# Seven half-size products for the first layer's projections, and the output gate's projection moved from the gated scan into the attention

## The chip, the cores and the metric

The kernel is one program on one core of a Trainium2 chip. Five engines work in it: TensorE (PE in the rows; PEld is its weight loads) multiplies matrices, VectorE (DVE), ScalarE (ACT) and GpSimd (POOL) work elementwise, and SyncE (SP) issues most of the DMAs. Each takes its instructions in order and waits on semaphores. The metric is the time of one execution in microseconds (us), the median of several runs. All data are fp32. An fp32 product leaves two records in the trace, so counts of records are twice the counts of products.

## What is computed

Two gated mixer layers are followed by a third block with state-space and delta-rule scans and an expert layer. The change touches the first half of the first layer, whose inputs are `x` (1024 tokens by 1024 channels) and one weight matrix:

```python
proj = jnp.einsum('bsd,df->bsf', h, w_in).astype(jnp.float32)
qa, ka, va, qb, kb, vb, lr_f, lr_b, gate = _split(
    proj, (A_WIDTH, A_WIDTH, A_WIDTH, B_K_WIDTH, B_K_WIDTH, B_V_WIDTH, B_GATE_RANK, B_GATE_RANK, MIX_WIDTH))
oa = dilated_attention(heads(qa, A_HEADS), heads(ka, A_HEADS), heads(va, A_HEADS), rel_bias)
g_f = jax.nn.log_sigmoid(lr_f @ up[0] + gb_[0]) / B_GATE_NORMALIZER
ob = bidirectional_gated_scan(qh, kh, heads(g_f, B_HEADS), kh, heads(g_b, B_HEADS), heads(vb, B_HEADS))
y = jnp.concatenate([oa, ob], axis=-1) * jax.nn.silu(gate)
```

The widths are 512 (qa, ka, va, qb, kb), 1024 (vb), 16 and 16 (the low-rank gates) and 1536 (the output gate). The attention has 8 heads of 64 in three dilations, the scan 4 heads in two directions over chunks of 32 tokens.

## The kernel before

The network is a row of stages; each ends with its last stores landed and a barrier. `xT` holds x with the 1024 input channels down the partitions, in 8 blocks, for the whole first layer. A unit of projection is 256 output columns. A job of kind CHANNEL writes channels down the partitions: the weights are stationary, 512 tokens move, 32 products a unit. A job of kind TOKEN writes tokens down the partitions: xT is stationary, 256 weight columns move, 64 products a unit.

1. `prologue` loads and transposes x and loads the first two units' weights.
2. `project` (tag `in0`) computes qa, ka (two CHANNEL units each) and va (two TOKEN units, stored into `vpad`), with TensorE alone at work and copies behind it.
3. `dilated_attention` (tag `att`) runs 96 slots: four pairs of heads, each with three dilations of eight tiles. In a slot TensorE turns the exponentials (line 1804), computes scores two slots ahead (line 1793) and the values of the slot before (line 1816), then takes a share of a `Background`: `low` (the low-rank gates, 32 columns), qb, kb and vb. Six of its fills come ahead of the first slot (`LEAD`). VectorE adds the bias (line 1854), takes three of the 256 "ada" products of the conditioning of a later block (lines 1866 and 1868), and moves the values out; ScalarE takes exponentials, copies `pT`, and copies the background's banks. SyncE issues the background's loads, the loads of two head pairs (20 DMAs each), three ada weight loads, and then the stores and loads of each slot in the order of its program.
4. `low_rank_scan` (tag `gla`) runs 32 steps: 4 heads of 8 tiles, both directions in a step. In TensorE's order a step is the update of the state (line 2121, needs ScalarE's copy `k_tok`), the output (lines 2134 and 2136), and the front of the next step: scores of 32-row tiles (line 2104, needs GpSimd's `queries`) and transposes of `k_end` (line 2111, needs VectorE). While head h is scanned, head h+1 is prepared: gates at steps 0 and 2 (line 2088) with ScalarE's logarithms behind them, cumulative sums by VectorE at steps 1 and 3, exponentials at steps 3 and 4, scaled queries at 5 and 6. The output gate (six TOKEN units, `gate_l0`) is a `Background` here: four leading fills between the first gates, and a share at three places of each step.
5. `close_layer` (tag `end0`) uses all of it.

The amount of a `Background` in a slot is set by a table made in its constructor: products times columns, spread evenly.

## Time and profile before

| | us |
|---|---|
| three runs, median (lowest to highest) | 4108.58 (4099.72 to 4109.97) |
| the profiled execution: its own time, its span | 4102.72, 4101.0 |
| TensorE busy over the span | 3579.0 (87%) |
| VectorE, ScalarE, GpSimd busy | 1812.7, 1081.5, 1183.6 |
| first projections, first to last product | 25.6 to 193.7 |
| attention, first background product to last value product | 207.2 to 684.8 |
| gated scan, first product to last | 695.5 to 1057.1 |
| mean granted clock of TensorE over the span (1 is 2.4 GHz, 0.5 is 1.2 GHz) | 0.924 |

Where a row of a timeline gives a duration, it runs from the start of the first record to the end of the last; products overlap their neighbours by some tenths, so the pace of a run of products is read from one start to the next. The time in brackets is the engine's idle time before the row, with what released it.

### The profile page before, as it was taken

What the parts mean: (1) busy time and instruction counts of PE and PEld (TensorE: products, weight loads), DVE (VectorE), ACT (ScalarE), POOL (GpSimd) and SP (SyncE); (2) the same over time, 40 slices, a digit from 0 to 9 for tenths busy, and PEclk for the clock granted to TensorE, in tenths of its full rate; (3) what the DMA queues carried; (4) which work ended last, traced back from release to release, by engine and by line L of the source; (5) the groups of instructions that cost most, each with busy time, mean ns of one, the idle gap of its engine ahead of it and who ended that gap; (6) DMA issues with size and microseconds to landing.
All of it is one profiled execution on the core that took longest, in us unless ns stands there. A gap on an engine that the chain in (4) does not pass through costs nothing. (4 is left out here: it accounts for less than half of the span.)

```text
span 4101.0 us, 47003 instructions
## 1 busy us (share of the span) xinstructions
PE 3579.0 (87%) x16369; PEld 2330.3 (57%) x16369; DVE 1812.7 (44%) x4038; ACT 1081.5 (26%) x2206; POOL 1183.6 (29%) x948
## 2 busy tenths in 40 slices
PE   8889998888798999999989598998966776949996
PEld 4645676667443676576647346665556775424442
DVE  0025552333374266566576352233478577241001
ACT  1023333333242233333342351221203212111111
POOL 0000000333243355555555353001303445211110
PEclk9999998899899999999999797998987888969998
DMA  3264532121532111211211633113234722346996
GB/s 115 72 176 147 160 118 85 61 97 57 195 147 86 53 56 50 60 55 50 59 51 36 240 140 81 45 43 117 90 101 128 254 91 75 144 181 232 318 322 230
DMA packets 409824, 494.01 MB, mean 120 GB/s; under 512 B 70514, under 2 KB 314506, under 8 KB 409603
## 3 DMA queue, kind: packets, MB, share of 16 engines
q1 hardware_dynamic: 380983, 457.42, 33.6%
q0 software_dynamic: 4608, 16.78, 1.6%
q10 hardware_dynamic: 24012, 16.97, 1.3%
q8 instruction: 126, 2.06, 0.2%
q14 instruction: 95, 0.78, 0.1%
HBM read 362.32 MB, written 128.77 MB: 120 GB/s over the span
## 5 line engine op out<-in xcount | busy, mean ns | idle before, releaser
L821 POOL TENSOR_TENSOR hgrn_queries<-hgrn_qd,hgrn_pair_decay 128x640 f32<-128x640 f32 x192 | 279.6, 1476 | 291.4 <-PE hgrn_ps_a L936 256.5
L395 PE MATMUL gla_bg_ps<-gla_bg_w,xT 128*128 128x256 f32 x768 | 199.8, 408 | 4.0 <-DMA gla_bg_w<-in_w_in_ab_dram 4.0
L871 PE MATMUL hgrn_ps_w<-xT,hgrn_ring 128*128 128x512 f32 x432 | 195.7, 599 | 1.8 <-PEq L34 1.8
L395 PEld LDWEIGHTS gla_bg_ps<-gla_bg_w,xT 128*128 128x128 f32 x768 | 154.3, 206 | 38.8 <-issue 11.0
L1473 PE MATMUL end_ps_z<-end_w,end_yT 128*128 128x512 f32 x384 | 168.7, 599 | 1.6 <-DMA end_w<-in_w_out_ab_dram 1.0
L2560 PE MATMUL end_ps_z<-end_w,end_yT 128*128 128x512 f32 x384 | 168.4, 598 | 0.8 <-ACT end_yT L2488 0.8
L391 PE MATMUL att_bg_ps<-xT,att_bg_w 128*128 128x512 f32 (+1 forms) x288 | 137.6, 618 | 13.3 <-POOL att_ident L1780 13.3
L45 POOL MEMSET gla_ident<- 128x128 f32 x1 | 0.2, 204 | 483.9 <-POOLq L34 483.9
L871 PEld LDWEIGHTS hgrn_ps_w<-xT,hgrn_ring 128*128 128x128 f32 x432 | 81.5, 193 | 94.3 <-issue 94.0
L871 PE MATMUL hgrn_ps_w<-hgrn_xs,hgrn_wsum 128*128 128x512 f32 x288 | 129.8, 598 | 5.3 <-ACT hgrn_sig L1153 5.3
L1041 DVE TENSOR_TENSOR hgrn_k_end<-hgrn_kd,hgrn_end_decay 128x128 f32<-128x128 f32 x168 | 127.3, 797 | 9.2 <-issue 2.6
L876 PE MATMUL hgrn_ps_w<-hgrn_ring,xT 128*128 128x256 f32 x576 | 128.8, 380 | 0.0
L2916 PE MATMUL in_ps<-hT_cols,in_w 128*128 128x512 f32 x288 | 126.2, 592 | 0.0
L2073 POOL TENSOR_TENSOR gla_queries<-gla_qd,gla_pair_decay 128x640 f32<-128x640 f32 x64 | 88.9, 1408 | 128.6 <-PE gla_ps_o L2136 91.3
L1473 PEld LDWEIGHTS end_ps_z<-end_w,end_yT 128*128 128x128 f32 x384 | 73.0, 192 | 92.5 <-issue 89.1
L2560 PEld LDWEIGHTS end_ps_z<-end_w,end_yT 128*128 128x128 f32 x384 | 73.1, 192 | 90.6 <-issue 89.4
L4776 PE MATMUL exp_ps_d<-expw_wd,exp_hidT 128*128 128x512 f32 x256 | 114.1, 599 | 11.0 <-ACT exp_hidT L4723 11.0
L395 PE MATMUL att_bg_ps<-att_bg_w,xT 128*128 128x256 f32 x512 | 123.4, 387 | 0.0
L1899 ACT ACTIVATE att_p_sb<-att_s_sb,att_shift 128x256 f32<-128x256 f32 (+1 forms) x192 | 88.8, 464 | 121.4 <-DVE att_shift L1858 121.3
L227 PE MATMUL in_ps<-xT,in_wbuf 128*128 128x512 f32 x256 | 113.0, 605 | 8.3 <-PEq L34 8.3
L876 PEld LDWEIGHTS hgrn_ps_w<-hgrn_ring,xT 128*128 128x128 f32 x576 | 108.0, 191 | 14.2 <-issue 0.5
L4758 PE MATMUL exp_ps_g<-expw_wg,exp_xT 128*128 128x512 f32 x256 | 115.3, 604 | 0.7 <-ACT exp_xT L4712 0.7
(645 smaller groups left out, 7700.9 us busy)
## 6 DMA issues: line engine op xcount, KB each, us to landing
expw_wg<-in_exp_w_gate_dram SPq DMA_DIRECT2D x16, 2048.0 KB, 10.3
expw_wu<-in_exp_w_up_dram SPq DMA_DIRECT2D x16, 2048.0 KB, 16.3
expw_wd<-in_exp_w_down_dram SPq DMA_DIRECT2D x16, 2048.0 KB, 21.9
att_w_ada<-in_ada_w_dram SPq DMA_DIRECT2D x24, 1024.0 KB, 6.4
hgrn_ring<-in_w_in_c_dram SPq DMA_DIRECT2D x18, 1024.0 KB, 5.4
end_gt<-gate_l SPq DMA_DIRECT2D x16, 768.0 KB, 8.5
hgrn_ring<-in_w_in_c_dram SPq DMA_DIRECT2D x24, 512.0 KB, 5.5
hgrn_o<-hgrn_o_stage SPq DMA_DIRECT2D x192, 64.0 KB, 1.6
```

What stands on the lines that cost most here:

```text
L227: last = pe.matmul(bank[0:job.rows, 0:job.span], w[:, k, b * job.rows:(b + 1) * job.rows], job.acts[:, k, s:s + job.span], start=(k == 0), ...
L391: last = pe.matmul(bank[0:job.rows, 0:job.span], w[:, k, b * job.rows:(b + 1) * job.rows], job.acts[:, k, s:s + job.span], start=(k == 0), ...
L395: last = pe.matmul(bank[0:job.rows, q * job.width:(q + 1) * job.width], job.acts[:, k, t * P:t * P + job.rows], w[:, k, 0:job.width], star ...
L821: pool.tensor_tensor(queries[:, d, s, :].rearrange("p (b a c) -> p b a c", b=POINTS, a=PC), q, f, ALU.mult).then_inc(queries_done, 1)
L871: last = pe.matmul(bank[:, :], a[:, k, :], x(k), start=(fresh and k == 0), stop=(k == HK - 1), skip_group_check=True)
L876: last = pe.matmul(bank[:, q * 2 * P:(q + 1) * 2 * P], x(k)[:, t * P:(t + 1) * P], a[:, k, :], start=(fresh and q == 0 and k == 0), stop=( ...
L1041: dve.tensor_tensor(k_end[:, d, p % 2, :].rearrange("p (a c) -> p a c", c=CH), kd[:, b, d, t * P:(t + 1) * P].rearrange("p (a c) -> p a c" ...
L1473: made = pe.matmul(ps_z[h][:, :], yT[:, k, :], w[:, k, h * BANK:(h + 1) * BANK], start=(k == 0), stop=(k == NB - 1))
L2560: made = pe.matmul(ps_z[h][:, :], yT[:, k, :], w[:, k, halves[h]], start=(k == 0), stop=(k == NB - 1))
L2916: last = pe.matmul(ps[(3 * n + part) % 2][:, 0:span], w[u % 3][:, k, b * P:(b + 1) * P], acts, start=(k == 0), stop=(k == KB - 1))
L4758: last = pe.matmul(ps_g[:, :], xT[:, b, k, :], wg[:, b, k, :], start=(k == 0), stop=(k == KB - 1))
L4776: last = pe.matmul(ps_d[g][:, :], hidT[:, j, :], wd[:, b, j, g * BANK:(g + 1) * BANK], start=(j == 0), stop=(j == FB - 1))
```

## The change

**Seven products.** A new class `Halves` takes the place of `project` in `in0` and of `Background` in the attention. It cuts the inner dimension, the 256 output columns and the 1024 tokens in two and computes the 2 by 2 blocks with seven half-size products (each 4 inner blocks deep) in place of eight. In token form the moving operand is now 128 weight columns wide, so a fill is 16 products; in channel form it stays 512 tokens and a fill is 4 products. The seven fills of a unit use three banks; four of them are copied to the stage by ScalarE (`move`), three are added to it by VectorE (`join`). GpSimd makes four sums of each unit's weights (`sums`), VectorE four sums of xT once, at the start of `in0`, the third in place.

**Where the work stands.** `low` is computed at the start of `in0`. The attention's background is qb, kb, vb and the six units of `gate_l0`, 14 units. The weights' ring of three units, the stage and the sums are shared by both stages; two of its units are loaded at the end of `in0`. The gated scan has no background. In the attention the ada weights come in pieces of 128 columns, six products a slot, three accumulators, and are loaded one slot later in relation to their use.

```diff
+UNIT_W = 256
+SNAP1, PLAIN, SNAP21, SNAP22, JOIN22, JOIN21, LAST = range(7)
...
+class Halves:
+    HK = KB // 2
+    ROLE = {SNAP1: 0, PLAIN: 1, SNAP21: 0, SNAP22: 2, JOIN22: 0, JOIN21: 2, LAST: 0}
+    PLACE = {SNAP1: 0, PLAIN: 0, LAST: 1, SNAP21: 2, JOIN21: 2, SNAP22: 3, JOIN22: 3}
+    BY_DVE = (PLAIN, JOIN22, JOIN21)
+    FRESH = (SNAP1, PLAIN, SNAP22)
+    DONE = (PLAIN, JOIN22, JOIN21, LAST)
...
+    def fetch(self, sp, g):
+        for f, end in enumerate(self.ended_in):
+            u, i = self.fills[f]
+            if end == g - 1 and i == LAST and u + self.RING < len(self.units):
+                self.load(sp, u + self.RING)
...
+    def put(self, sp, g):
+        for f, end in enumerate(self.ended_in):
+            if end == g - 2 and self.fills[f][1] in self.DONE:
+                self.store(sp, f)
...
+    def sums(self, pool, u):
+        a, s = self.weights_of, self.wsum
+        wait(pool, self.w_loaded[u % self.RING], self.loads_by[u])
+        wait(pool, self.filled, 7 * u)
+        pool.tensor_tensor(s[:, 0, :, :], a(u, 0, 0), a(u, 1, 0), ALU.subtract).then_inc(self.s_made, 1)
+        pool.drain()
+        pool.tensor_tensor(a(u, 1, 0), a(u, 1, 0), a(u, 1, 1), ALU.add).then_inc(self.s_made, 1)
+        pool.drain()
+        pool.tensor_tensor(s[:, 1, :, :], a(u, 1, 0), a(u, 0, 0), ALU.subtract).then_inc(self.s_made, 1)
+        pool.drain()
+        pool.tensor_tensor(s[:, 2, :, :], a(u, 0, 1), s[:, 1, :, :], ALU.subtract).then_inc(self.s_made, 1)
...
+    def multiply(self, pe, g, x_made=None):
+        for f, lo, hi in self.work[g]:
+            u, i = self.fills[f]
+            bank, w, x = self.ps[self.bank_of[f]], self.stationary(u, i), self.x[i]
+            if lo == 0:
+                if i == SNAP1:
+                    wait(pe, self.w_loaded[u % self.RING], self.loads_by[u])
+                e = self.before_on[f]
+                if e is not None:
+                    pe.wait_ge(self.added if self.fills[e][1] in self.BY_DVE else self.moved, self.nth[e])
+                if x_made is not None and u == 0 and i in (SNAP21, JOIN22, JOIN21):
+                    pe.wait_ge(x_made, {SNAP21: 2, JOIN22: 3, JOIN21: 4}[i])
+                if i in (SNAP21, LAST):
+                    pe.wait_ge(self.s_made, 4 * u + (3 if i == SNAP21 else 4))
+            for n in range(lo, hi):
+                q, k = n // self.HK, n % self.HK
+                if self.units[u].kind == CHANNEL:
+                    last = pe.matmul(bank[:, :], w[:, k, :], x(k), start=(i in self.FRESH and n == 0), stop=(k == self.HK - 1), skip_group_check=True)
+                else:
+                    last = pe.matmul(bank[:, q * P:(q + 1) * P], x(k)[:, q * P:(q + 1) * P], w[:, k, :],
+                                     start=(i in self.FRESH and n == 0), stop=(k == self.HK - 1), skip_group_check=True)
+            if hi == self.count(f):
+                last.then_inc(self.filled, 1)
...
+    def move(self, act, g):
+        for f, end in enumerate(self.ended_in):
+            u, i = self.fills[f]
+            if end != g - 1 or i in self.BY_DVE:
+                continue
+            place = self.PLACE[i]
+            act.wait_ge(self.filled, f + 1)
+            wait(act, self.stored[place], 16 * u)
+            act.activation(self.stage[:, place, :], self.ps[self.bank_of[f]][:, :], ACT.Copy).then_inc(self.moved, 1)
+    def join(self, dve, g):
+        for f, end in enumerate(self.ended_in):
+            u, i = self.fills[f]
+            if end != g - 1 or i not in self.BY_DVE:
+                continue
+            into = self.stage[:, self.PLACE[i], :]
+            snap = f + {PLAIN: SNAP1, JOIN22: SNAP22, JOIN21: SNAP21}[i] - i
+            dve.wait_ge(self.filled, f + 1)
+            dve.wait_ge(self.moved, self.nth[snap])
+            dve.tensor_tensor(into, self.ps[self.bank_of[f]][:, :], into, ALU.add).then_inc(self.added, 1)
...
+            seven.load(sp, 2)
+            sp.wait_ge(low_moved, 2)
+            sp.dma_start(low_out, low[:, :, :].rearrange("p s t -> p (s t)")).then_inc(low_stored, 16)
+            for g in range(seven.slots):
+                seven.transfer(sp, g)
+                for n, unit in enumerate(ahead):
+                    if g == 7 * (len(units) - 3 + n) + 7:
+                        sp.wait_ge(seven.filled, g)
+                        src = unit.weights.rearrange("(k p) n -> p k n", p=P)[:, :, unit.col:unit.col + UNIT_W]
+                        sp.dma_start(ring[:, n, :, :], src).then_inc(ahead_loaded, 16)
+            seven.end(sp)
+            sp.wait_ge(low_stored, 16)
+            sp.wait_ge(ahead_loaded, 16 * len(ahead))
+        @block.gpsimd
+        def _(pool):
+            for u in range(len(units)):
+                seven.sums(pool, u)
+        @block.tensor
+        def _(pe):
+            for s in range(2):
+                for k in range(KB):
+                    last = pe.matmul(ps_l[s][0:2 * RANK, :], low_w[:, k, :], xT[:, k, s * BANK:(s + 1) * BANK], start=(k == 0), stop=(k == KB - 1))
+                last.then_inc(low_made, 1)
+            for g in range(seven.slots):
+                seven.multiply(pe, g, x_made)
...
-    ADA_W = 256
+    ADA_W = 128
+    PER = 6
...
-        bg = Background(sb, sem, pbank, jobs, HEADS * ST, 3, 3, 3, lead=LEAD)
+        bg = Halves(sem, xT, xs, ring, wsum, bg_stage, [pbank(f"bg_ps{b}") for b in range(3)], units, HEADS * ST, 2, lead=LEAD)
...
-            return unit_ends[u] // 3 + 2
+            return unit_ends[u] // PER + 1
...
-            return range(3 * g, min(3 * g + 3, len(PRODUCTS)))
+            return range(PER * g, min(PER * g + PER, len(PRODUCTS)))
...
-            bg.begin(sp)
             sp.wait_ge(consts, 1)
             load(0)
+            bg.load(sp, 2)
             load(1)
             load_ada(0)
             load_ada(1)
@@ -1753,8 +1999,8 @@
                 bg.transfer(sp, g)
             for g in range(HEADS * ST):
                 bg.transfer(sp, LEAD + g)
-                if g + 1 in unit_due and unit_due[g + 1] + 3 < ADA_UNITS:
-                    load_ada(unit_due[g + 1] + 3)
+                if g in unit_due and unit_due[g] + 3 < ADA_UNITS:
+                    load_ada(unit_due[g] + 3)
...
+            for u in range(len(units)):
+                bg.sums(pool, u)
...
+                bg.join(dve, g)
...
+                bg.join(dve, LEAD + g)
...
                 for half in range(2):
                     gate(0, d, half)
-                bg.multiply(pe, 2 * d)
-                bg.multiply(pe, 2 * d + 1)
-            bg.multiply(pe, LEAD)
             front(0)
             for g in range(STEPS):
                 h, p = g // TILES, g % TILES
-                if g:
-                    bg.multiply(pe, LEAD + 3 * g)
                 if p < CARRIED:
                     update(g)
                 if h + 1 < heads and p in (0, 2):
                     gate(h + 1, p // 2, 0)
-                bg.multiply(pe, LEAD + 3 * g + 1)
                 output(g)
                 if h + 1 < heads and p in (0, 2):
                     gate(h + 1, p // 2, 1)
-                bg.multiply(pe, LEAD + 3 * g + 2)
                 if g + 1 < STEPS:
                     front(g + 1)
...
-            with ExitStack() as first_weights:
-                wbuf = [first_weights.enter_context(nc.sbuf_tensor(f"in0_wbuf{b}", [P, KB, 256], F32)) for b in range(2)]
-                prologue(nc, "pro", x[0], xT, rel_bias, buckets, vectors, vpad, c_2, c_ctx_2, sT, w, wbuf)
-                project(nc, "in0", [
-                    Job(CHANNEL, xT, SEQ, w, 0, 256, 2, qa),
-                    Job(CHANNEL, xT, SEQ, w, A, 256, 2, ka),
-                    Job(TOKEN, xT, SEQ, w, 2 * A, 256, 2, vpad[VPAD:VPAD + SEQ, :]),
-                ], loaded=wbuf)
-            dilated_attention(nc, "att", qa, ka, vpad, vectors, attn, [
-                Job(CHANNEL, xT, SEQ, w, 5 * A + B, 2 * RANK, 1, low),
-                Job(CHANNEL, xT, SEQ, w, 3 * A, 256, 2, qb),
-                Job(CHANNEL, xT, SEQ, w, 4 * A, 256, 2, kb),
-                Job(TOKEN, xT, SEQ, w, 5 * A, 256, 4, vb),
-            ], sT, ada_w_2[0], ada)
-            low_rank_scan(nc, "gla", 4, B // 4, qb, kb, vb, low, gla_gate_up[0], gla_gate_bias[0], gla_o, 1 / 16, scale, [
-                Job(TOKEN, xT, SEQ, w, 5 * A + B + 2 * RANK, 256, 6, gate_l0),
-            ])
+            low_at = 5 * A + B
+            channels = lambda col, dst: [Unit(CHANNEL, w, col + UNIT_W * n, dst, UNIT_W * n) for n in range(A // UNIT_W)]
+            tokens = lambda col, dst, width: [Unit(TOKEN, w, col + UNIT_W * n, dst, UNIT_W * n) for n in range(width // UNIT_W)]
+            first = channels(0, qa) + channels(A, ka) + tokens(2 * A, vpad[VPAD:VPAD + SEQ, :], A)
+            second = channels(3 * A, qb) + channels(4 * A, kb) + tokens(5 * A, vb, B) + tokens(low_at + 2 * RANK, gate_l0, A + B)
+            with ExitStack() as shared:
+                held = lambda n, *shape: shared.enter_context(nc.sbuf_tensor(n, [P, *shape], F32))
+                ring, wsum = held("l0_ring", 3, KB, UNIT_W), held("l0_wsum", 3, KB // 2, P)
+                stage, xs = held("l0_stage", 4, BANK), held("l0_xs", 3, KB // 2, BANK)
+                with nc.sbuf_tensor("l0_low_w", [P, KB, 2 * RANK], F32) as low_w:
+                    prologue(nc, "pro", x[0], xT, rel_bias, buckets, vectors, vpad, c_2, c_ctx_2, sT, w, ring, low_w, low_at)
+                    project_halves(nc, "in0", xT, xs, ring, wsum, stage, first, second[0:2], low_w, low)
+                dilated_attention(nc, "att", qa, ka, vpad, vectors, attn, xT, xs, ring, wsum, stage, second, sT, ada_w_2[0], ada)
+            low_rank_scan(nc, "gla", 4, B // 4, qb, kb, vb, low, gla_gate_up[0], gla_gate_bias[0], gla_o, 1 / 16, scale)
```

At the start of the attention TensorE's order before is this (`att_bg_ps` are the background's banks, `att_ps_s` the scores, `att_ps_t` the transposes, `att_ps_o` the values):

```order
L391 MATMUL att_bg_ps<-xT,att_bg_w 32x512 x16
L391 MATMUL att_bg_ps<-xT,att_bg_w 128x512 x32
L1793 MATMUL att_ps_s<-att_k,att_q 128x256 x4
L1804 MATMUL att_ps_t<-att_ident,att_p_sb 128x128 x4
L1793 MATMUL att_ps_s<-att_k,att_q 128x256 x2
L391 MATMUL att_bg_ps<-xT,att_bg_w 128x512 x3
L1804 MATMUL att_ps_t<-att_ident,att_p_sb 128x128 x4
L1793 MATMUL att_ps_s<-att_k,att_q 128x256 x2
L1816 MATMUL att_ps_o<-att_v,att_pT 128x64 x4
L391 MATMUL att_bg_ps<-xT,att_bg_w 128x512 x2
```

and after (`l_ring` holds weights, `l_wsum` their sums, `l_xs` the sums of xT):

```order
L559 MATMUL att_bg_ps<-xT,l_ring 128x512 x8
L559 MATMUL att_bg_ps<-l_xs,l_wsum 128x512 x8
L559 MATMUL att_bg_ps<-xT,l_ring 128x512 x4
L559 MATMUL att_bg_ps<-l_xs,l_ring 128x512 x4
L2041 MATMUL att_ps_s<-att_k,att_q 128x256 x4
L2052 MATMUL att_ps_t<-att_ident,att_p_sb 128x128 x4
L2041 MATMUL att_ps_s<-att_k,att_q 128x256 x2
L559 MATMUL att_bg_ps<-xT,l_wsum 128x512 x4
L2052 MATMUL att_ps_t<-att_ident,att_p_sb 128x128 x4
L2041 MATMUL att_ps_s<-att_k,att_q 128x256 x2
```

The leading fills are 24 products of 512 columns in place of 48 (16 of them for 32 channels), and a slot's share is four in place of two or three.

In a step of the gated scan, from the transposes of one front to the next front, TensorE's order before is:

```order
L2111 MATMUL gla_ps_k<-gla_ident,gla_k_end 128x128 x2
L395 MATMUL gla_bg_ps<-gla_bg_w,xT 128x256 x4
L2121 MATMUL gla_ps_u<-gla_v_in,gla_k_tok 128x256 x2
L395 MATMUL gla_bg_ps<-gla_bg_w,xT 128x256 x3
L2134 MATMUL gla_ps_o<-gla_v_in,gla_scores 128x256
L2136 MATMUL gla_ps_o<-gla_state,gla_queries 128x256
L2134 MATMUL gla_ps_o<-gla_v_in,gla_scores 128x256
L2136 MATMUL gla_ps_o<-gla_state,gla_queries 128x256
L395 MATMUL gla_bg_ps<-gla_bg_w,xT 128x256 x3
```

and after:

```order
L2355 MATMUL gla_ps_k<-gla_ident,gla_k_end 128x128 x2
L2365 MATMUL gla_ps_u<-gla_v_in,gla_k_tok 128x256 x2
L2378 MATMUL gla_ps_o<-gla_v_in,gla_scores 128x256
L2380 MATMUL gla_ps_o<-gla_state,gla_queries 128x256
L2378 MATMUL gla_ps_o<-gla_v_in,gla_scores 128x256
L2380 MATMUL gla_ps_o<-gla_state,gla_queries 128x256
```

The three pieces of `gla_bg_ps` are gone; between the last transpose and the update nothing stands now. In the same way the four gates of the stage's opening stand together, where 32 background products stood between the first pair and the second.

On SyncE's queue, behind the loads of the first two head pairs, there stood:

```order
L1729 DMA att_w_ada<-in_ada_w_dram 128x8x256 x3
L347 DMA low<-att_bg_stage 32x512
L336 DMA att_bg_w<-in_w_in_ab_dram 128x8x256
L347 DMA low<-att_bg_stage 32x512
L347 DMA qb<-att_bg_stage 128x512 x3
L336 DMA att_bg_w<-in_w_in_ab_dram 128x8x256
L347 DMA qb<-att_bg_stage 128x512 x2
```

and there stands:

```order
L1975 DMA att_w_ada<-in_ada_w_dram 128x8x128 x3
L507 DMA qb<-l_stage 128x512 x3
L488 DMA l_ring<-in_w_in_ab_dram 128x8x256
L507 DMA qb<-l_stage 128x512
L1975 DMA att_w_ada<-in_ada_w_dram 128x8x128
L507 DMA qb<-l_stage 128x512
L1975 DMA att_w_ada<-in_ada_w_dram 128x8x128
```

The ada loads are half as wide. The background's first loads, three units ahead of the head pairs before, are one unit between the two pairs now.

## Rows read from the trace of the kernel before

**Rows 1.** Windows, all engines: us, busy time (records), granted clock, DMA share, GB/s.

```profile
40.00:137.00 97.00, 97.00 (x227) 42.94 (x226) 4.84 (x7) 4.18 (x7) 0.00 (x0) 1.00 0.21 65
139.00:193.00 54.00, 54.00 (x252) 47.54 (x251) 2.41 (x4) 2.39 (x4) 0.00 (x0) 1.00 0.18 59
207.20:251.20 44.00, 44.00 (x96) 15.88 (x96) 0.00 (x0) 1.77 (x3) 0.00 (x0) 0.94 0.97 255
251.20:685.20 434.00, 424.17 (x2097) 288.20 (x2096) 213.89 (x832) 169.79 (x536) 0.00 (x0) 0.99 0.40 119
747.90:1056.50 308.60, 272.41 (x1574) 214.90 (x1575) 109.99 (x304) 95.48 (x146) 100.56 (x68) 0.93 0.22 71
1000.00:1056.50 56.50, 56.50 (x362) 47.98 (x361) 12.49 (x54) 9.24 (x18) 12.42 (x10) 1.00 0.16 57
```

**Rows 2.** Timeline, TensorE: start us, us, operation, count; 128-column products.

```profile
2897.99 1.50 PE L3397 MATMUL gdnp_ps_r<-gdnp_mask,logs 128*128 128x128 f32 x12
2899.33 2.74 PE L391 MATMUL gdnp_bg_ps<-hT,gdnp_bg_w 128*128 128x512 f32 x6
```

**Rows 3.** Timeline, SyncE's queue, then TensorE: start of the attention.

```profile
222.44 0.43 SPq L1698 DMA_DIRECT2D att_q<-qa  x1
240.25 6.20 SPq L1729 DMA_DIRECT2D att_w_ada<-in_ada_w_dram  x3
...
261.30 1.11 PE L1804 MATMUL att_ps_t<-att_ident,att_p_sb 128*128 128x128 f32 x4 [7.37 <-ACT att_p_sb L1899]
```

**Rows 4.** Groups, shapes apart: count | busy us, mean ns | idle before, releaser.

```profile
L395 PE MATMUL gla_bg_ps<-gla_bg_w,xT 128*128 128x256 f32 x768 | 199.8, 408 | 4.0 <-DMA gla_bg_w<-in_w_in_ab_dram 4.0
...
L762 POOL TENSOR_TENSOR hgrn_wsum<-hgrn_ring 128x512 f32<-128x512 f32 x18 | 22.9, 1270 | 80.3 <-PE hgrn_ps_w L871 41.0 <-PE hgrn_ps_w L876 35.4 <-POOLq L34 3.8
...
L283 DVE COPY in_stage<-in_ps 128x512 f32<-128x512 f32 x12 | 8.3, 691 | 167.9 <-PE in_ps L227 115.4 <-PE in_ps L233 52.5
```

**Rows 5.** Timeline, three engines: opening of the gated scan.

```profile
705.06 16.85 PE L395 MATMUL gla_bg_ps<-gla_bg_w,xT 128*128 128x256 f32 x64 [4.00 <-DMA gla_bg_w<-in_w_in_ab_dram]
...
705.41 1.06 ACT L2287 ACTIVATE gla_mag<-gla_mag 128x1024 f32<-128x1024 f32 x1
...
706.58 1.23 DVE L2173 SCALAR_TENSOR_TENSOR gla_cum<-gla_z,gla_mag 128x1024 f32<-128x1024 f32 x1 [21.41 <-ACT gla_mag L2287]
```

**Rows 6.** Timeline, TensorE, then ScalarE: a step of the last head.

```profile
1011.91 0.49 PE L2104 MATMUL gla_ps_s<-gla_queries,gla_kd 128*32 128x128 f32 x16
1012.33 0.44 PE L2111 MATMUL gla_ps_k<-gla_ident,gla_k_end 128*128 128x128 f32 x2
...
1014.34 1.03 PE L2121 MATMUL gla_ps_u<-gla_v_in,gla_k_tok 128*128 128x256 f32 x4
...
1016.50 0.59 PE L2134 MATMUL gla_ps_o<-gla_v_in,gla_scores 128*128 128x256 f32 x2
...
1018.23 1.46 PE L395 MATMUL gla_bg_ps<-gla_bg_w,xT 128*128 128x256 f32 x6
...
1012.81 0.38 ACT L2305 ACTIVATE gla_k_tok<-gla_ps_k 128x256 f32<-128x256 f32 x1 [1.00 <-PE gla_ps_k L2111]
```

**Rows 7.** Timeline, TensorE, then ScalarE: steps 0 to 4 of the second head.

```profile
847.42 1.13 PE L2121 MATMUL gla_ps_u<-gla_v_in,gla_k_tok 128*128 128x256 f32 x4 [1.70 <-ACT gla_k_tok L2305]
...
858.33 0.69 PE L2111 MATMUL gla_ps_k<-gla_ident,gla_k_end 128*128 128x128 f32 x2 [5.05 <-DVE gla_k_end L2223]
...
876.55 1.13 PE L2121 MATMUL gla_ps_u<-gla_v_in,gla_k_tok 128*128 128x256 f32 x4 [2.98 <-ACT gla_k_tok L2305]
...
885.56 0.44 PE L2111 MATMUL gla_ps_k<-gla_ident,gla_k_end 128*128 128x128 f32 x2 [1.46 <-DVE gla_k_end L2223]
...
869.60 0.69 ACT L2279 ACTIVATE gla_z<-gla_ps_z,gla_shift 128x512 f32<-128x512 f32 x1 [0.46 <-PE gla_ps_z L2088]
```

**Rows 8.** Windows, all engines: two stretches in which the granted clock fell.

```profile
858.30:864.20 5.90, 5.87 (x15) 4.33 (x15) 0.54 (x5) 0.38 (x1) 0.00 (x0) 0.50 0.00 0
3100.00:3216.00 116.00, 87.08 (x630) 82.64 (x628) 102.06 (x215) 46.25 (x85) 29.39 (x52) 0.88 0.54 171
```

144 lines of the change are left out of this document (120 added, 24 removed).

## The prediction

> **What bounds the kernel now.** The windows by stage come first [rows 1]. In the first projections TensorE is busy in the whole of both clean stretches, and in the attention for 424.17 of 434.0 us; both stages last as long as TensorE's work. In the gated scan it is busy for 272.41 of 308.6 us, 36 us idle, so the scan is bounded by TensorE only as long as the projections behind it are there. The sum is therefore made from TensorE records for the first two stages and from the scan's own chain for the third. An fp32 product leaves two records.
>
> **Price of a record** [rows 1, 2]. 512 columns: 97.0 us / 227 = 0.427 us. 256 columns: 54.0 / 252 = 0.214 us. The new token products move 128 columns, of which the first layer has none in a row; the nearest is the run of 12 records of the same shape at 2897.99, behind which the next line starts at 2899.33: 1.34 / 12 = 0.112 us. So per column 256 and 128 cost nearly the same, and the load of 128 weight columns before each product stays hidden in that run.
>
> **What a unit of 256 output columns costs.** Channel form: 32 products (64 records) of 512 before, 27.3 us; 7 x 4 products (56 records) now, 23.9 us; 3.4 us less. Token form: 64 products (128 records) of 256 before, 27.4 us; 7 x 16 products (224 records) of 128 now, 25.1 us; 2.3 us less. The low-rank gate's 32 channels are not halved: two fills of 8 products, 32 records, 13.7 us.
>
> **First projections.** Four channel units and two token units give back 4 x 3.4 + 2 x 2.3 = 18.2 us, and the low-rank projection comes in for 13.7: -4.5. VectorE's sums of xT and GpSimd's sums of weights are new and lie under it: SNAP21, the first product that wants them, stands 13.7 us plus two products of 3.4 us into the stage. The 128 KB load ahead of the ring I take at +1 us, the end of the stage (stores of 256 KB in place of 1 MB) at -1.5. Sum -5, between -8 and +5 (a late sum in one unit).
>
> **Attention.** The low-rank projection goes (-13.7), four channel and four token units are halved (-13.6 - 9.2), and the six output gate units come in at 25.1 us each (+150.5): +114.0 us of TensorE work in a stage that is TensorE's. It is all on the path. What else changes is the start. The leading fills shrink from 48 products (44.0 us, [rows 1]) to 24 of 0.854 us, 20.5 us. Before, that time hid SyncE's issues: the first pair of heads lands under it, the second pair is issued from 222.44 to 240.2, and only then the first three ada weights [rows 3]. VectorE takes its ada products between bias(0) and bias(1), and TensorE's score(2), third in its order, waits for bias(1). Counted from the stage's start at 207.2, the ada weights are issued 33.0 us in and land some 6 us later (the page's median for this load is 6.4 us), so with VectorE's 3 us of products and bias score(2) starts at about 42 us. Before, the transposes behind which it stands started 54.1 us in, after 7.37 us of waiting for ScalarE, whose queue held copies for `low` and `qb` with stores still to come [rows 3]. The fills, first scores and first transposes now end at about 24 us, so TensorE idles some 18 us against some 9, less what is left of ScalarE's own waits for stores: +7 (0 to +12). Attention: +121 (+112 to +130).
> Cover of the other additions: VectorE is busy 213.9 of 434.0 us of this stage [rows 1]. 42 joins at 0.69 us (a copy of the same 128x512 [rows 4]) add 29 us; the ada products in twice as many halves cost between nothing more and as much again, at most 214 us. That is under 460 of some 570 us: hidden. GpSimd's four sums per unit (1.27 us each [rows 4]) have two fills, 7 us, before the first is wanted. SyncE passes more entries, and the 24 issues of a load of a pair now stand before ada loads of 1.3 slots' worth; with three buffers I take nothing, and 5 us at the high end.
>
> **The gated scan.** 768 records of 256 columns leave [rows 4], 164 us of TensorE. What is left is a chain. The opening: the second pair of gate products stood behind 64 background records, from 705.06 to 721.9, while ScalarE had finished the first logarithm at 706.5 and VectorE the step behind it at 707.8 [rows 5], all that the pair needs. It moves up by 14 us, and the exponentials, keys and queries that follow it as well: -14.
> A step of the last head takes 56.5 / 8 = 7.1 us now [rows 1]. The rows of one [rows 6] without the background: front 0.42, transposes to ScalarE's copy and update 0.91 (1012.33 to 1013.19, and a wait's 0.06), update 0.86, output 1.73: 3.9 us. The last head runs at this: 6 such steps, the short first and last: 28 us, against 56.5.
> In the other three heads the chain is longer, and these waits do not shrink with TensorE's work [rows 7]. After the gates of steps 0 and 2 ScalarE takes the logarithms before it copies the keys: 6.95 us from 869.60 to the update at 876.55, 5.7 where one table load is less. In steps 1 and 3 VectorE builds the cumulative sums between the state and the next k_end: 10.9 us from the update at 847.42 to the transposes at 858.33, 9.0 from 876.55 to 885.56. Walking one head from its first update: gates and output 4.0, logarithms 5.7, sums 10.9, transposes to update 0.9, gates and output 4.8, logarithms 7.0, sums 9.0 + 0.9, output and exponentials 5.7 (an estimate, from 1.06 us for each of ScalarE's two wide passes [rows 5]), scaled queries and k_end 5.3 + 0.9 (an estimate, from VectorE's 1.23 us for a wide pass), last output, front and transposes 6.8: 62 us, of which TensorE works 30. Before, the three heads took (308.6 - 56.5) / 3 = 84 us each. Loop: 3 x 62 + 28 + 2 = 216.
> Then the clock. In 858.3 to 864.2, right behind 5.05 us of idle, the granted clock was 0.50, the lower of the two levels; and from 3100 to 3216, where TensorE is busy 75% with VectorE at its heels, its mean is 0.88 [rows 8]. The new heads have four such idle stretches each. All their work at the lower level would add some 21 us per head (only what is on the chain); I take a third, 7 each, +21. Loop 237 against 308.6: -72 (216 to 279: -93 to -30). Scan: -86 (-107 to -44).
>
> **Sum.** -5 + 121 - 86 = +30 against the profiled execution's 4102.7 (span 4101.0 and 1.7 around it), so 4133 there; that run lies 6 us below the median of 4108.6, which puts the forecast at 4138 as a median. TensorE's records sum to -4.5 + 114 - 164 = -55 us: the work does shrink, but what leaves the scan had hidden the scan's own waits, and what arrives in the attention hides nothing.
>
> **Rivals.**
> The waits overlap (ends at no change). For it: the walk above adds ScalarE's and VectorE's waits end to end, and the one sum took 10.9 us and the other 9.0; if the clock stays and 3 us go from each sum, the loop is about 200 to 210, the total about 4108 + 30 - 30 = 4108. Against it: program order puts the logarithms, the key copy, the update and the sums one behind the other.
> The scan shrinks by all its background (ends faster). The loop would keep TensorE's 272 us less 632 x 0.214 = 137: -171 in place of -72, total 4039; every loop below about 190 us gives a gain of more than 0.3%. For it only that TensorE is the busiest engine there; against it the idle rows themselves, up to 5.05 us with 4.3 us of background per step before them. Decides: a head with preparation below 53 us.
> The clock stays low (slower still). If the three heads run at the lower level throughout, loop 279, total 4180.
> The 128-column products cost more in long runs. Each 0.01 us on a record is 12 units x 224 x 0.01 = 27 us. For it: no long run of this shape with changing weights is in the trace; against it the run of 12 without a gap. At 0.12 the total is about 4160.
> The Trainium skill, TensorE: Matmul & The Clock Gate, section Back-to-back issue gap, speaks against so small a product: in a stream of weight loads and matmuls it gives about 81 ns at 128 columns and 131 ns at 512, so that a quarter of the columns costs 0.62 of the time. By that ratio a record of 128 would be 0.26 us and the twelve token units some 400 us dearer; the trace does not agree (0.112 against 0.427, a ratio of 0.26).
> VectorE or SyncE bounds the attention (slower). If ada products, joins and GpSimd's sums on a shared path reach TensorE's pace in one slot of four, some 25 us: 4160.
>
> **How the numbers follow.** The forecast, +30 with a spread of 12 from clock and start, has 0.50. No change by overlapping waits 0.18, faster by a short loop 0.11, clock low throughout 0.08, dearer 128-column products 0.06, VectorE or SyncE in the attention 0.07. 0.3% is 12 us and about what a measurement of this kernel can tell from no change. Of the forecast's 0.50 some 0.04 lies below +12. Slower 0.46 + 0.21 = 0.67, same 0.22, faster 0.11. The range 4098 to 4178 leaves out the short loop and the far end of the clock.
>
> **What would show it.** Right: attention from first fill to last about 599 us with TensorE near 97% busy after the start, its first wait of some 15 us before score(2); 128-column records 0.112 us apart; scan steps of 3.9 us in the last head and heads of 62 to 69 us before it, with TensorE waiting for gla_k_tok and gla_k_end; the second gate pair 14 us earlier. Wrong: waits on `s_made` or `added` in the projections, TensorE idle behind VectorE in the attention's slots, a scan head below 53 or above 80 us.

## The result and the profile after

The changed kernel takes 4185.65 us (median of 4 runs, 4178.16 to 4187.43) against 4108.61 us for the kernel before in the same runs: a ratio of 1.0187, 95% interval 1.0171 to 1.0204. The forecast was 4138 us with a range to 4178. The direction was right, the size was not: 77 us slower where 30 were forecast, and outside the range.

By stage, in the two profiled executions (us):

| stretch | before | forecast | after |
|---|---|---|---|
| attention's first product, from the span's start | 207.2 | 202 | 200.9 |
| attention, first to last product | 477.7 | 599 | 623.1 |
| scan, first product to first update | 54.2 | 40 | 39.4 |
| scan, the three heads with preparation | 86.5, 81.1, 82.5 | 69 each | 80.2, 77.7, 74.8 |
| scan, last head | 57.3 | 28 | 30.5 |
| everything behind the scan | 3043.9 | 3044 | 3047.5 |

So 24 us of the miss lie in the attention and 26 us in the three heads of the scan. (The row behind the scan, whose stages are the same in all kernels here, ran from 3037.6 to 3050.6 us over the profiled executions of this document, so totals carry some us that have nothing to do with an edit, and a stage's own length is the better measure.)

The windows of the changed kernel that answer to [rows 1] (us; busy time and records of TensorE, weight loads, VectorE, ScalarE, GpSimd; granted clock; DMA share; GB/s), first a pure stretch of 128-column products in the first projections, then the attention, then the four heads of the scan:

```profile
141.00:189.00 48.00, 48.00 (x432) 48.00 (x431) 4.15 (x6) 4.18 (x7) 9.14 (x8) 1.00 0.30 89
...
200.90:824.00 623.10, 589.57 (x3904) 457.88 (x3904) 328.28 (x1129) 185.43 (x585) 71.94 (x56) 0.97 0.43 121
874.89:955.09 80.20, 49.39 (x239) 31.06 (x239) 35.00 (x82) 25.94 (x37) 29.85 (x21) 0.66 0.11 36
955.09:1032.75 77.66, 46.49 (x239) 29.86 (x239) 34.86 (x82) 25.94 (x37) 26.15 (x18) 0.69 0.17 54
1032.75:1107.58 74.83, 44.74 (x238) 29.18 (x239) 33.81 (x82) 25.94 (x37) 28.29 (x19) 0.70 0.17 57
1107.58:1138.10 30.52, 26.31 (x212) 19.73 (x212) 13.05 (x54) 6.48 (x13) 14.99 (x13) 1.00 0.20 70
```

Three things are to be seen. The 128-column record costs 48.00 / 432 = 0.111 us in a long run too. In the attention TensorE is idle for 33.5 us (9.5 before). And in the three heads the clock is 0.66 to 0.70 (0.94 before over the loop), where the last head, whose idle stretches are of 0.4 to 0.7 us, has 1.00.

What TensorE waited for, in the attention and then in the three heads (us in total, times, longest):

```profile
PE att_ps_s L2041 <- DVE att_shift L2106: 32.5, 16, 17.6
```

```profile
PE gla_ps_k L2355 <- DVE gla_k_end L2460: 44.8, 9, 9.1
PE gla_ps_u L2365 <- ACT gla_k_tok L2542: 44.3, 19, 6.2
```

The longest of the attention's waits is the one that was forecast. The timeline of SyncE's queue and TensorE (it answers to [rows 3]; start, us, what, and in brackets the idle time before it) shows it:

```profile
227.58 7.12 SPq L1957 DMA_DIRECT2D att_tab<-vectors  x12
234.74 5.80 SPq L1975 DMA_DIRECT2D att_w_ada<-in_ada_w_dram  x3
...
245.83 1.23 PE L2041 MATMUL att_ps_s<-att_k,att_q 64*128 64x256 f32 x4 [17.61 <-DVE att_shift L2106]
```

score(2) runs 45.0 us after the stage's first product, behind 17.6 us of idle; the forecast had 42 and some 18. The other 14.9 us in 15 waits were not forecast. One of them, VectorE and TensorE (the transposes began at 392.71):

```profile
392.91 0.69 DVE L587 TENSOR_TENSOR l_stage<-att_bg_ps,l_stage 128x512 f32<-128x512 f32 x1 [3.94 <-PE att_bg_ps L561]
393.52 0.41 DVE L2102 CUSTOM_DVE_ANT_0 att_s_sb<-att_ps_s,att_tab 128x256 f32<-128x256 f32 x1
...
394.59 0.70 PE L2041 MATMUL att_ps_s<-att_k,att_q 64*128 64x256 f32 x4 [1.28 <-DVE att_shift L2106]
```

`att_bg_ps` L561 is the last background product of the slot. VectorE had been idle for 3.94 us with the scores of the next bias ready, but the join (0.69 us) stands ahead of that bias in its order; join and bias together are longer than TensorE's transposes, and score waits 1.28 us.

### The profile page after: what moved, and what is told of

Read it like the earlier page. It is cut to its first block and busy times, and to the rows that moved or that the text cites. A ratio compares the mean times of both kernels' runs of the same rounds, so it can differ in the third digit from the quotient of the medians.

```text
span 4185.6 us, 50213 instructions
## 1 busy us (share of the span) xinstructions
PE 3564.0 (85%) x17505; PEld 2352.4 (56%) x17505; DVE 1953.0 (47%) x4346; ACT 1091.8 (26%) x2242; POOL 1286.7 (31%) x1028
## 5 line engine op out<-in xcount | busy, mean ns | idle before, releaser
L529 POOL TENSOR_TENSOR l_wsum<-l_ring 128x512 f32<-128x512 f32 x20 | 27.7, 1383 | 645.2 <-PE att_bg_ps L561 356.2
L2116 DVE SCALAR_TENSOR_TENSOR att_acc<-att_w_ada,sT,att_acc 128x128 f32<-128x128 f32 x448 | 175.8, 413 | 26.9 <-issue 0.9
L561 PE MATMUL att_bg_ps<-l_ring,xT 128*128 128x128 f32 x960 | 119.4, 280 | 0.0
L2041 PE MATMUL att_ps_s<-att_k,att_q 64*128 64x256 f32 (+1 forms) x384 | 91.5, 559 | 32.6 <-DVE att_shift L2106 32.5
L1301 DVE COPY_PREDICATED hgrn_scores<-hgrn_mask,hgrn_ps_s 128x128 f32<-128x128 uint32 x192 | 48.8, 298 | 148.0 <-issue 147.9
L561 PEld LDWEIGHTS att_bg_ps<-l_ring,xT 128*128 128x128 f32 x960 | 112.8, 194 | 5.4 <-issue 5.4
## 6 DMA issues: line engine op xcount, KB each, us to landing
expw_wd<-in_exp_w_down_dram SPq DMA_DIRECT2D x16, 2048.0 KB, 21.5
```

Of the source, the lines that this page charges most:

```text
L561: last = pe.matmul(bank[:, q * P:(q + 1) * P], x(k)[:, q * P:(q + 1) * P], w[:, k, :], start=(i in self.FRESH and n == 0), stop=(k == self ...
L2041: last = pe.matmul(ps_s[h][:, 0:wide(d)], queries(q[:, b, :], d, t, rows), keys(k[:, b, :], d, t, rows), start=True, stop=True)
L2116: last = dve.scalar_tensor_tensor(out=mine, in0=w, scalar=s, in1=mine, op0=ALU.mult, op1=ALU.add)
```

## The experiments

All times are medians of 4 to 10 runs (x12: 2), and ratios are to the kernel before as it ran beside each kernel. There it took 4101 to 4103 us, where beside the changed kernel it had taken 4108.61 us; so the distance of a total from the changed kernel's 4185.65 us can be some 6 us too large. Where a stage's length is given, it is the safer number.

### The attention: two orders

x4 moves the three ada loads ahead of the second pair of heads:

```
             bg.load(sp, 2)
-            load(1)
             load_ada(0)
             load_ada(1)
             load_ada(2)
+            load(1)
```

> The changed kernel with one edit: on SyncE's queue of the attention the three ada loads stand before the loads of the second pair of heads, not behind them. Theory: score(2)'s wait of 17.6 us is the queue's issue time; it falls to 2 us or less, attention 623 - 16 = 607 us, total 4170 us. Rival: the wait is the landing of the first pair and of the weights, for which the transfers share the DMA engines; then half of it stays, total 4178 us.

Measured: 4167.93 us. The wait of 17.6 us is 1.7 us; the attention is 11.6 us shorter, not 16: ScalarE makes the transposes wait 1.9 us once, and half-clock stretches at 227.9 to 231.3 and 248.4 to 255.2 us now fall on work, where the stretch of 230.5 to 251.0 us had fallen mostly on idle time. The mechanism stands.

x5 puts the joins behind the next bias:

```
                 bias(g)
+                if g:
+                    bg.join(dve, LEAD + g - 1)
                 ...
                 if g > 1:
                     move_out(g - 2)
-                bg.join(dve, LEAD + g)
+            bg.join(dve, LEAD + HEADS * ST - 1)
             bg.join(dve, LEAD + HEADS * ST)
```

> The changed kernel with one edit: VectorE's joins stand behind the bias of the next slot, not ahead of it, so that no bias waits for the last product of a fill. Theory: of the attention's 32.5 us of waits of score for VectorE, the 17.6 us of the start stay and the six of 1.28 us and most of the smaller ones go: attention -9 to -12 us, total 4175 us. Rival: those waits come from VectorE's load (ada products, GpSimd's sums beside them), and the order changes nothing: 4186 us.

Measured: 4169.24 us, attention 623.1 to 612.1 us. What is left of the waits is the start and one of 3.7 us. Ahead of that one VectorE waits 5.1 us for the DMA of the ada weights (`att_w_ada`) and then takes 4.25 us for three ada products beside GpSimd's sums, where two took 0.78 us just before. In the whole attention:

```profile
PE att_ps_s L2041 <- DVE att_shift L2106: 23.5, 3, 18.5
```

The term that the prediction lacked is this order: 11 us. (The rest of the 16 us of the total isn't the edit's: in the profiled executions the scan is 3 us shorter and the stages behind it 6 us, none of which the edit touches.)

### The halving alone

x2 leaves the six gate units in the scan's background, in their old form and with the scan as before:

```
-            second = channels(3 * A, qb) + ... + tokens(5 * A, vb, B) + tokens(low_at + 2 * RANK, gate_l0, A + B)
+            second = channels(3 * A, qb) + ... + tokens(5 * A, vb, B)
```

> The halving alone: the changed kernel with the six gate units left in the gated scan's background in their old form. xT is restored there by one sum on VectorE (128 x 2048) before the first product. My theory: first projections -6 us, attention 477.7 - 36.5 of TensorE work + 10 for the start + 8 for waits behind joins = 459 us, gated scan 362 to 365 us as before: 4108.6 - 6 - 19 + 2 = 4086 us, faster than before by 0.5%. Rival: the shorter slots put VectorE (ada products, joins) on the path in the first 86 slots and the gain is gone: 4100 to 4112 us.

Measured: 4126.66 us, ratio 1.0059 (1.0037 to 1.0080): slower than before, where 0.5% faster was expected, and worse than the rival. The scan is nearly as before (359.1 us for 361.7). The attention has by the prices of the records 36 us less to multiply than before and takes 513.5 us, 36 us more:

```profile
198.90:712.40 513.50, 459.74 (x2560) 319.62 (x2560) 305.81 (x1111) 173.37 (x561) 40.99 (x32) 0.92 0.44 122
```

```profile
PE att_ps_s L2041 <- DVE att_shift L2106: 46.8, 26, 19.1
```

With 96 slots of 5.3 us, where the changed kernel has 6.5, there are 25 waits for VectorE beyond the start, 27.7 us, one of 6.0 us for ScalarE, and the clock falls to 0.92. Is it VectorE's load or its order? x9 leaves out three quarters of the ada products, x7 mends the orders (the edits of x4 and x5) and keeps the load. The edit of x9:

```
+                if 0 < kb < KB - 1:
+                    return
                 mine, w, s = acc[:, u % 3, r, :], w_ada[:, u % 3, kb, :], sT[:, kb, r:r + 1]
```

> The halving alone (gate units left in the scan, old form) with VectorE's ada products left out but for the first and last of each eight, so the ada values are not the reference's (128 of 512 products are left, some 160 us less for VectorE). Theory: VectorE's load bounds the slots of this attention, 27.7 us of waits beyond the start, with the half-clock stretches behind them. Without it the attention falls from 513 to 470 us, total 4083 us. Rival: the waits come from the order of join and bias alone; then they stay: 4115 to 4126 us.

> The halving alone (gate units left in the scan, old form), with both edits in the attention: ada loads before the second pair of heads, joins behind the next bias. The halving alone took 4126.7 us. Theory: both edits give back what they give in the changed kernel, 17 us at the start and 10 to 12 us in the slots: 4098 us, a little under the kernel before. Rival: in these shorter slots (5.0 us) VectorE is the bound whatever its order, the second edit gives nothing: 4110 us.

Measured: 4105.51 us for x9, 4083.94 us for x7.

| attention | us | score(2)'s wait for VectorE, all other waits for it | VectorE busy | clock |
|---|---|---|---|---|
| x2, halved | 513.5 | 19.1, 27.7 | 305.8 | 0.92 |
| x9, without most ada products | 484.1 | 18.7, 16.0 | 166.3 | 0.95 |
| x7, both orders mended | 466.5 | 1.1, 16.0 | 305.7 | 0.97 |
| x11 (below), the attention of x7 | 474.5 | 1.4, 15.5 | 305.8 | 0.95 |

Both experiments missed in size: x9 gave 21 us of 44 expected, x7 gave 43 of 29. The two are not to be compared as they stand, because x7 makes two edits. The one on SyncE's queue takes 18 us of score(2)'s wait away, which x9 keeps. On the other waits the second edit, the place of the joins, and the load that x9 leaves out do the same: 27.7 us become 16.0 in both. So in these short slots VectorE's load counts as well as its order, and which of them makes the 16 us that stay was not tested; no run has the load away and the orders mended. The length is 29 us less with x9, and 39 to 47 us less with x7's orders: x7 and x11 run the same attention with nearly the same waits and differ by 8 us, at a clock of 0.97 and 0.95. With both edits the halving beats the kernel before, ratio 0.9960 (0.9946 to 0.9974).

### The move alone

x1 is the kernel before with the gate units appended to the attention's jobs in their old form, and the changed scan:

```
                 Job(TOKEN, xT, SEQ, w, 5 * A, 256, 4, vb),
+                Job(TOKEN, xT, SEQ, w, 5 * A + B + 2 * RANK, 256, 6, gate_l0),
```

> The move alone: the kernel before, with the six output gate units put at the end of the attention's background in their old form (64 products of 256 columns each), and the changed kernel's gated scan without background. Nothing is halved. My theory: the stages add up. Attention 477.7 us + 6 x 27.4 = 642 us with the start as before (no wait of 17 us before score(2), no waits behind joins), gated scan 302 us as in the changed kernel, so 4108.6 + 164 - 59 = 4214 us, and the halving is then worth about -27 us in the changed kernel. Rival: the halving itself costs (its joins on VectorE, its sums on GpSimd, the 128-column products), then this kernel is at or below the changed one's 4186 us.

Measured: 4211.24 us, ratio 1.0266 (1.0248 to 1.0283). Attention 642.6 us (642 expected), scan 303.3 us. The move costs 108 us: the attention pays all 165 us of the gate's products, the scan gives back 58 of the 164 us that it loses. Halving then gives back 26 us by the medians (31 us by each kernel's distance from the kernel before beside it), about half of the 55 us of TensorE work that it saves by the prices of the records.

### The scan: clock and chain

x3 and x6 put unread products where TensorE waits. They read constant tiles and write a bank of their own:

```
+            def fill(n):
+                for _ in range(n):
+                    pe.matmul(ps_f[:, 0:2 * P], ident[:, :], mask[:, :, :], start=True, stop=True)
```

> The changed kernel with products in the gated scan whose result nobody reads, placed where TensorE waits: 20 in the opening, then in each head but the last 6, 6 and 4 before the update of steps 1, 3 and 5 and 8, 8 and 3 before the transposes of steps 2, 4 and 6; 125 products of 256 columns in all, 54 us at the full clock. Theory of the clock: the loop of 263 us is long because TensorE's clock is at the lower level in most of it; with the work in the waits the clock stays up, and the loop falls to some 235 us although TensorE does more: 4186 - 28 = 4158 us. Rival, ScalarE's and VectorE's chain alone: heads of 75 to 80 us whatever the clock, so the loop stays at 263 us or grows by what the products overshoot the waits: 4186 to 4205 us.

> The kernel with unread products in the gated scan's waits, with more of them: 44 in the opening, then in each head but the last 10, 10 and 5 before the update of steps 1, 3 and 5 and 14, 20 and 6 before the transposes of steps 2, 4 and 6; 239 products of 256 columns, 102 us at the full clock. With 125 of them the clock in the three heads rose from 0.69 to 0.83 and the loop fell by 6 us. Theory of the clock: the rest of the low stretches goes too, clock above 0.95 in the three heads, heads of 68 to 70 us, loop 240 us, total 4162 us. Rival, the chain of ScalarE and VectorE: heads stay at 74 us or more with the clock up, total 4175 to 4190 us.

Measured: 4178.69 us with 125 products, 4166.40 us with 239. The first head, 80.2 us at 0.66 in the changed kernel (874.89:955.09 above), takes 77.6 us at 0.80 in x3, and in x6:

```profile
873.98:944.98 71.00, 63.58 (x368) 47.18 (x369) 37.13 (x82) 25.94 (x37) 29.09 (x19) 0.95 0.13 43
```

x3 moved the loop by 6 us, not 28: waits of up to 6.5 us are left in it, and the clock is still at 0.80 to 0.84. x6 shows the clock's share: at 0.93 to 0.95 the three heads take 71.0, 70.9 and 71.3 us, so what x6 gives back of the clock is worth 77.6 - 71.1 = 6.5 us a head. More products, less time. But 71 is not the 62 us of the walk.

x10 and x12 ask what VectorE's sums cost in such a head. In x6, as in the changed kernel, GpSimd's product of the next keys starts among VectorE's small sums. The changed kernel's rows:

```profile
1003.51 2.34 POOL L2302 TENSOR_TENSOR gla_kd<-gla_k_in,gla_rel 128x1024 f32<-128x1024 f32 x1 [15.07 <-ACT gla_rel L2531]
1003.71 2.19 DVE L2431 TENSOR_TENSOR gla_ends<-gla_totals,gla_points 128x32 f32<-128x32 f32 x1 [0.43 <-issue]
```

In the kernel before, in the step that the prediction walked, the same product began after the sums were over, and the same sum of 32 elements took 0.19 us, not 2.19:

```profile
884.09 0.19 DVE L2194 TENSOR_TENSOR gla_ends<-gla_totals,gla_points 128x32 f32<-128x32 f32 x1
...
886.42 2.35 POOL L2058 TENSOR_TENSOR gla_kd<-gla_k_in,gla_rel 128x1024 f32<-128x1024 f32 x1 [15.34 <-ACT gla_rel L2294]
```

In the changed kernel the sum ends at 1005.90 us and GpSimd's product at 1005.85 (start and duration added), so the sum did not run slowly but waited for the whole product. The Trainium skill, SBUF — State Buffer, section Who interferes with whom, has a rule for it: the port pair that VectorE and GpSimd share is an exclusive lock, and a VectorE instruction with two inputs in SBUF contends with a GpSimd instruction that reads SBUF. The trace agrees.

x10 issues the keys one step later (`p in (6, 7)` in place of `(5, 6)`); x12 cuts them to 32 columns in the preparation of the last two heads (`m = SEQ if h < 2 else CH`), which leaves their keys wrong. Both are x6 otherwise.

> The kernel with 239 unread products (4166.4 us, heads of 71.0 us at a clock of 0.95), with one edit: GpSimd scales the next head's keys one step later in its order (behind the queries of steps 6 and 7, not 5 and 6). In it VectorE's small sums of the second direction are stretched beside GpSimd's wide products: the sum of 32 elements takes 2.18 us, the ends 0.91 and the last addition 1.23 us, where the same three take 0.19, 0.19 and 0.33 us undisturbed. Theory: this collision is 3 to 4 us of each head, the step of 13.9 us falls to 10.5, heads to 67.5 us, total 4156 us. Rival: the keys are then late for the next head, whose first step waits for them, and the gain is given back: 4166 us or more.

> The kernel with 239 unread products (4166.4 us, heads of 71.0, 70.9 and 71.3 us), with GpSimd's product that scales the next head's keys cut from 1024 to 32 columns for the third and the fourth head (prepared in the second and third), so those keys are not the reference's; the first head prepares the second in full and is the control within the run. Theory of the collision: VectorE's sums of the second direction are then stretched only by the queries' products, and the step of 13.9 to 14.3 us falls by 2 to 3 us in the second and third head and stays in the first. Rival: the sums take what they take, and GpSimd's product is off the path: all three steps stay at 13.9 us.

Measured: 4167.77 us for x10, no gain. GpSimd's products still fell among VectorE's instructions, only among others:

```profile
991.42 4.57 POOL L2318 TENSOR_TENSOR gla_queries<-gla_qd,gla_pair_decay 128x640 f32<-128x640 f32 x2 [8.55 <-PE gla_ps_o L2387]
991.75 3.18 DVE L2420 TENSOR_TENSOR_SCAN gla_cum<-gla_starts,gla_cum 128x1024 f32<-128x1024 f32 x1
...
995.00 2.07 DVE L2427 TENSOR_TENSOR gla_rel<-gla_cum 128x1024 f32<-128x1024 f32 x1
996.24 3.04 POOL L2303 TENSOR_TENSOR gla_kd<-gla_k_in,gla_rel 128x1024 f32<-128x1024 f32 x1 [0.24 <-issue]
997.00 2.35 DVE L2429 TENSOR_TENSOR gla_to_mid<-gla_cum 128x32 f32<-128x32 f32 x1
```

Undisturbed these take 2.48 us (two products), 2.29, 1.23, 2.34 and 0.2 us. Their ends, start and duration added, show the engines taking turns: the second product of queries ends 1.1 us behind VectorE's scan, `gla_rel` 1.1 us behind that product, the keys 2.2 us behind `gla_rel`, and the sum 0.1 us behind the keys. Each waits for the whole of the other's instruction and then takes about its own time.

x12 (4163.53 us, two runs) has the control in itself: the step took 14.5 us in the first head and 12.8 in the other two, whose whole length is 68.3 us against 71. So the keys' product costs up to 3 us a head. In the step itself 1.1 to 1.7 us show, less than the 2 to 3 expected, but here the experiment limits itself: the 20 unread products end only at 994.6 us, 1.3 us after `k_end` is ready at 993.3 (2.1 us earlier in its step than in x6), and the transposes stand behind them. The collision with the keys is thus worth about 2 us of the step. The rest of the head goes with the clock (0.97 to 0.98 for 0.95) and wasn't separated.

x8 changes only the order on two queues of the scan: on VectorE k_end goes ahead of the sums, on ScalarE the logarithms go behind the next step's key copy.

```
+                early = p in (1, 3)
+                if early:
+                    scale_keys(h, p + 1)
                 if h + 1 < heads:
                     prepare(h + 1, p)
-                if g + 1 < STEPS and (g + 1) % TILES < CARRIED:
+                if not early and g + 1 < STEPS and (g + 1) % TILES < CARRIED:
                     scale_keys((g + 1) // TILES, (g + 1) % TILES)
...
                     move_keys(h, p)
                 more = h + 1 < heads
+                if more and p in (1, 3):
+                    logs(h + 1, p // 2)
...
                     gate(h + 1, p // 2, 1)
-                    logs(h + 1, p // 2)
```

> The changed kernel with another order in the gated scan, no work added or taken away: in steps 1 and 3 VectorE makes the next step's k_end ahead of the sums, and ScalarE takes the logarithms behind the key copy of the following step. Theory, the orders of these two queues are the chain that bounds a head: TensorE's waits for gla_k_tok and gla_k_end (29.5 us a head) shrink, some come back as waits for scores and state; heads from 77.6 to 71 us, loop 263 to 243 us, total 4167 us. Rival: the work of ScalarE and VectorE is the chain in any order, the waits only change their name: 4180 to 4187 us.

Measured: 4144.47 us, 41 us less (39 in the loop), twice the expected gain. Heads of 67.9, 61.9 and 63.6 us, with the clock still at 0.72 to 0.81. The waits of the three heads:

```profile
PE gla_ps_u L2365 <- ACT gla_k_tok L2545: 32.7, 19, 6.7
PE gla_ps_o L2378 <- DVE gla_scores L2471: 31.2, 9, 5.3
```

The 44.8 us for k_end are 4.2 us; 31 us came back as waits for the scores, as the theory had it. With the same work on every engine a head is 13 us shorter: what held a head at 77.6 us was the order of the queues, not the engines' work alone.

### Versions

x11 is x7 with x8's order in its scan, x13 the changed kernel with all three orders mended, x14 the kernel before with x8's order alone.

> The halving alone with both edits in the attention (4083.9 us), and the same reordering in its gated scan, where the gate's projections still run behind the steps. Theory: TensorE waits 36 us there, 20 for gla_k_end and 15 for gla_k_tok; a third to a half goes, loop 306 to 291 us, total 4069 us. Rival: the waits only change their name: 4084 us.

> The changed kernel with all three orders mended: ada loads first, joins behind the next bias, and the scan's k_end ahead of the sums with the logarithms behind the next key copy. Alone they gave -18, -16 and -41 us against 4185.7. Theory, they lie in separate places and add up by the stages (attention -12 - 11, scan -39): 4185.7 - 62 - some 5 of spread = 4120 us, still above the kernel before, since the gate's projections hide nothing in the attention: 55 us above x11, which differs in their place alone. Rival: with the waits mended the place no longer matters and it comes to the 4065 to 4085 us of the others.

> The kernel before with the scan's reordering alone. Theory: it gives the same 19 us as on the halving alone (4083.9 to 4065.2), since the scan and its background are the same: 4102 - 19 = 4083 us. Rival: nothing, if the gain there came from the restored xT or the attention's other end: 4100 us.

| kernel | median us | ratio to before (95%) |
|---|---|---|
| x13, changed, orders mended | 4120.87 | 1.0046 (1.0029 to 1.0063) |
| x14, before, scan's order | 4076.46 | 0.9943 (0.9927 to 0.9960) |
| x11, halved, gate in the scan, all orders | 4065.21 | 0.9907 (0.9891 to 0.9924) |

The orders add up as expected (4120 forecast for x13). x11 and x13 differ in the place of the gate's projections (and their form): 56 us. x14 shows that most of x11's gain has nothing to do with the change: the reorder gives 25 us to the kernel before (22 us in the scan's loop, 19 expected), the halving with its attention mended another 11 us. x11 beats both kernels, by 0.9% and 2.9%.

## The prediction, step by step

- **Price of a record, units.** Right. 0.111 us at 128 columns in a run of 432 records; the rival of dearer 128-column products falls. The prediction's ratio of 0.62, an estimate from the Trainium skill (TensorE: Matmul & The Clock Gate, section Back-to-back issue gap), would have made it 0.26 us; the trace disagrees in a long run as well.
- **First projections, -5.** Right: -6.3 us, no wait on `s_made` or `added`.
- **Attention, +121.** Measured +145.4. The price of the move was right (x1, in the old form: 642.6 us for 642). The start was right in size, with some luck: 17.6 us of idle for 18, because both its ends came 3 us later than forecast (27.4 and 45.0 us for 24 and 42). Two terms were wrong. "42 joins at 0.69 us ... hidden" failed: it summed VectorE's busy time over the stage and found room, but a join at the slot's end stands ahead of the bias for which score waits. That is 11 us (x5); the one wait of 3.7 us that x5 leaves has late ada weights and GpSimd's sums before it. And TensorE's busy time grew by 121.4 us, not 114. Of this some 2 us are twice as many sums `att_ps_a` for ada units of half the width (96 records for 48, together 18.3 us for 16.0 from start to start), which had no term; part is the clock (0.97 for 0.98), and the rest wasn't separated.
- **Opening, -14.** Right: -14.8 us.
- **Last head, 28 us.** 30.5: steps of 4.1 us for 3.9; update and output are 0.2 us longer than in the one step they were read from.
- **The head of 62 us.** This step failed. With the clock at 0.95 a head takes 71 us. Its parts by update to update, forecast and x6: steps 0 and 1 together 21.5 and 21.6; step 2 11.8 and 15.4; step 3 9.9 and 13.9; the last three 18.7 and 20.1. Step 3 rested on sums without GpSimd beside them, as the kernel before had them. In x6 three small sums of this step wait for GpSimd: they take 2.18, 0.91 and 1.23 us for 0.19, 0.19 and 0.33, 3.6 of the 4.0 us. Step 2 is no fault of the walk but of the clock: the logarithms take their 7.0 us, and the 3.6 us are gates and outputs at the lower level, after the preceding wait (967.6 to 974.4 us). The last three steps' 1.4 us stay open.
- **The clock, 7 us a head.** Too small. x6 gives back 6.5 us between 0.68 and 0.95, and the 3.6 us of step 2 that it leaves belong to the clock too: some 10 us a head. The clock is low for most of a head, but much of that time is idle, and idle time doesn't get longer with it: the bound of 21 us a head did not come. So of the 8.6 us that a head (77.6 us) lies above the forecast's 69, about 5.5 are the walk and 3 the clock.
- **Sum.** First projections -6, attention +145, scan -59 and some +4 between and behind the stages make the +84.6 of the profiled executions, for +30. Both misses went the same way. The range held a slow scan or a slow attention, not both.
- **Rivals.** "The waits overlap" and "the scan shrinks by its background" fell: no head came below 68 us while the queues kept their order. "The clock stays low" gave 4180 us and came nearest to the total, by luck: its loop was 279 us and its attention 599, measured were 263 and 623. "VectorE in the attention" was the right place. It named VectorE's load; in the changed kernel the order of one small step was worth 11 us with the load as it was (x5), while in the shorter slots of the halving alone the load counts as well (x9). Its path through the shared ports shows in one wait of 3.7 us.

## To carry to other kernels

Work that runs behind waits costs only part of its time, and work moved to a stage that is full costs its whole price: here 165 us paid for 58 us back. Before such a move, look at why the waits are there; the order of two queues in the scan was worth 25 us with the work left where it was. When an engine gets a small step in a slot's sequence, don't only ask whether its busy time leaves room, but what stands behind that step and who waits for it. And look whether an experiment's own filler has become the bound before its result is read as the size of an effect (x12).

## What the chip showed that was not expected

- A VectorE sum of 32 elements per partition takes 0.19 us alone and 2.19 us when it meets a GpSimd product of 128x1024. Large instructions wait for each other in the same way, in both directions (x10): VectorE's scan of 1024 elements takes 3.18 for 2.29 us, two GpSimd products of 128x640 take 4.57 for 2.48 us, and the chain of ends shows that they take turns by whole instructions.
- 239 products that nobody reads, 102 us of TensorE work at the full clock, went with a scan's loop that is 19 us shorter (263.2 to 243.8 us), at a mean clock of 0.95 for 0.72.
- Waits of 1 to 3 us in the attention of x2 came with half-clock stretches of 3 to 7 us behind them (0.92 on average), so a wait cost more than itself: x7 took away 29 us of idle time (53.8 to 25.2) and the stage became 47 us shorter. Where such a stretch falls is not fixed by the program alone: x7 and x11 have the same attention and nearly the same waits, and are 8 us apart (0.97 and 0.95).
